# Routing a mixture of experts by comparing logits at once, with the common path behind the branch made the one that falls through

## The reference, cut to what matters

```python
def hierarchical_moe(h, w_rg, b_rg, w_re, b_re, w_e_gate, w_e_up, w_e_down):
    ...
    p_grp = jax.nn.softmax((t @ w_rg + b_rg).astype(jnp.float32), axis=-1)
    g_val, g_idx = lax.top_k(p_grp, 1)
    le = (t @ w_re + b_re).astype(jnp.float32).reshape(n, MOE_GROUPS, EXPERTS_PER_GROUP)
    le_sel = jnp.take_along_axis(le, g_idx[:, :, None], axis=1)[:, 0]
    p_exp = jax.nn.softmax(le_sel, axis=-1)
    e_val, e_idx = lax.top_k(p_exp, EXPERT_TOP_K)
    e_val = e_val / jnp.sum(e_val, axis=-1, keepdims=True)
    weight = g_val * e_val
    ...
```

## Time and profile before

| | |
|---|---|
| median of 3 runs | 1658.11 us (1657.22 to 1660.17) |
| profiled execution, first to last instruction | 1655.9 us |
| PE, DVE, ACT busy | 1530.4, 1093.5, 705.5 us |
| last xo matmul starts | 1392.08 us |
| first expert matmul starts | 1429.11 us |
| mean granted clock of TensorE | 0.988 |

### The profile page before, as it was taken

The page is one execution under the profiler, slowest core; times in us unless marked ns, Lnnn a source line. Parts: engine busy times, 40 slices in busy tenths (PEclk is TensorE's granted clock), DMA queues, the critical chain, the costliest instruction groups (busy, mean ns, idle before and its releaser), DMA issues.

```text
span 1655.9 us, 26753 instructions
## 1 busy us (share of the span) xinstructions
PE 1530.4 (92%) x11012; PEld 1284.9 (78%) x11012; DVE 1093.5 (66%) x1661; ACT 705.5 (43%) x1057; POOL 57.3 (3%) x52
## 2 busy tenths in 40 slices
PE   5999988998999999999999999999999888788892
PEld 4889777876878888888878787787898667788892
DVE  5831776686499637637689997455765445677775
ACT  5422444443344333323454222234344346367773
POOL 0000000000000000000000000000000000232121
PEclk9999999999999999999999999999999999999996
DMA  6220000002412222222312222232243103688995
GB/s 249 102 94 9 2 3 3 2 3 78 170 59 102 81 98 102 102 102 85 119 56 98 102 98 81 102 115 102 77 153 134 70 26 112 212 273 324 333 343 209
DMA packets 37832, 189.74 MB, mean 115 GB/s; under 512 B 4305, under 2 KB 4433, under 8 KB 24401
## 3 DMA queue, kind: packets, MB, share of 16 engines
q1 hardware_dynamic: 30672, 167.08, 28.1%
q0 software_dynamic: 4864, 16.78, 2.8%
q10 hardware_dynamic: 2176, 4.19, 0.8%
HBM read 175.46 MB, written 12.58 MB: 114 GB/s over the span
## 4 chain that ended last, share of the span: by engine, by line
PE 70%; DVE 17%; DMA 4%; ACT 4%; issue 3%; POOL 0%; SPq 0%; POOLq 0%; DVEq 0%; ACTq 0%
PE acc L474 18%; PE acc L476 18%; PE acc L475 18%; DMA raw<-wstream 3%; DVE CA L2439 2%; PE acc L725 2%; PE mb L725 1%; DVE wl L1958 1%; DVE wl L1970 1%; ACT wh L1254 1%; PE acc L1032 1%; PE mb L556 1%; DVE sqa L1887 1%; PE mb L610 1%; ACT wh L1267 1%
## 5 line engine op out<-in xcount | busy, mean ns | idle before, releaser
L474 PE MATMUL acc<-XH,wh 128*128 128x512 f32 x1008 | 396.3, 393 | 2.2 <-DVE wl L1970 1.3
L476 PE MATMUL acc<-XH,wl 128*128 128x512 f32 x1008 | 392.4, 389 | 0.0
L475 PE MATMUL acc<-XL,wh 128*128 128x512 f32 x1008 | 392.2, 389 | 0.0
L1267 ACT ACTIVATE wh<-raw 128x2048 fp32r<-128x2048 f32 x99 | 189.3, 1914 | 242.0 <-DMA raw<-wstream 242.0
L1970 DVE TENSOR_TENSOR wl<-raw,wh 128x2048 fp32r<-128x2048 f32 x99 | 226.1, 2287 | 67.2 <-ACT wh L1267 64.0
L474 PEld LDWEIGHTS acc<-XH,wh 128*128 128x128 f32 x1008 | 189.2, 188 | 44.6 <-issue 3.2
L475 PEld LDWEIGHTS acc<-XL,wh 128*128 128x128 f32 x1008 | 189.2, 188 | 40.8 <-issue 1.9
L476 PEld LDWEIGHTS acc<-XH,wl 128*128 128x128 f32 x1008 | 189.2, 188 | 39.6
L1288 ACT ACTIVATE ev<-acc 128x512 f32<-128x512 f32 x146 | 85.5, 597 | 216.7 <-PE acc L476 187.2
L1958 DVE TENSOR_TENSOR wl<-raw,wh 128x1024 fp32r<-128x1024 f32 x96 | 116.5, 1223 | 39.7 <-ACT wh L1254 39.3
L1254 ACT ACTIVATE wh<-raw 128x1024 fp32r<-128x1024 f32 x96 | 100.7, 1059 | 32.1 <-DMA raw<-wstream 31.7
(11 more groups left out here) (533 smaller groups left out, 2768.2 us busy)
## 6 DMA issues: line engine op xcount, KB each, us to landing
raw<-wstream SPq DMA_DIRECT2D x99, 1024.0 KB, 4.8
raw<-wstream SPq DMA_DIRECT2D x96, 512.0 KB, 6.1
YG<-YT ACTq DMA_DIRECT2D x8, 512.0 KB, 6.0
XT<-xT SPq DMA_DIRECT2D x2, 1024.0 KB, 9.7
XT<-xT SPq DMA_DIRECT2D x1, 2048.0 KB, 7.8
XD<-HN SPq DMA_DIRECT2D x4, 512.0 KB, 2.6
out<-XTK SPq DMA_DIRECT2D x4, 512.0 KB, 2.6
cst<-consts SPq DMA_DIRECT2D x1, 1230.0 KB, 18.5
```

The costliest lines, as they stand in the source:

```text
L474: mm(out_, a[0], b[0], start=start, stop=False)
L475: mm(out_, a[0], b[1], start=False, stop=False)
L476: return mm(out_, a[1], b[0], start=False, stop=stop)
L1267: actv(wh[:, n % RING].rearrange("p a b c -> p (a b c)"), raw[:, n % RING, :], ACT.Copy).then_inc(hi_done, 1)
```

## The change: what it does

1. **Routing.** All four-way comparisons of all 20 logits are made at once: differences `beat` (128x320), a comparison with a small tie-breaking constant, a sum that counts by how many an entry is beaten. Entries beaten by none (groups) or at most one (experts) are taken; `chosen` is the product of the two masks. No softmax is needed for it. The weights follow later from exponentials of the group logits and of the difference of the two experts' logits (`exponents` inside `place_first`, `two_weights` after `place(1)`). Weights for the dense path are made in that path.
2. **Last block of xo.** Tile 6 runs over all k, then routers 4 and 5, then tile 7. Tile 7 is added by DVE straight from PSUM. The low part of the third expert block of weights is made before tile 7 instead of after the choice.
3. **Transposes of the tokens.** They go in pairs of banks of `acc`, interleaved with the router; the first ones come before the logits' transposes, the last ones before the count. The stores to `XD` take two tiles of half the features each.
4. **Count and placing.** 6 matmuls for 14 in the count; `rows_in` of an expert is now cast before the next `G1` is begun; the flag is made after the first `G1`; the copies `pcur` go.
5. **Before the branch** only slot (0, 0) is turned and split, ahead of `slot_rows(1)`; the others follow one per block in `gathered(0)`, blocks 0 to 4. `keep_busy` there is 4 for 6.
6. **The branch.** Condition and bodies are swapped on PE, ACT and DVE: the common path falls through, the dense one is jumped to, and the common path jumps over it at its end. ACT's table for Silu is loaded before the branch.

```diff
-            for b in range(4):
+            for b in range(3):
                 stage_blocks("xo", 1, (s["xs_done"], 1) if b == 0 else None, start=b)
...
+            begin_block(n, t)
+            for j in range(2):
+                for k in range(KT):
+                    last = mm3(acc[:, (t + j) % 4, :], (wh[:, n % RING, k, j, :], wl[:, n % RING, k, j, :]),
+                               (XH[:, k, :], XL[:, k, :]), k == 0, k == KT - 1)
+                last.then_inc(acc_ready, 1)
+                if j == 0:
+                    router(4)
+                    router(5)
             router(6)
...
+            pe.wait_ge(s["rx_g"], 8)
+            for p in (2, 3):
+                pe.wait_ge(s["f_toke"], 2 * p - 2)
+                turned_row(p, 0)
+                turned_row(p, 1).then_inc(s["f_tok"], 2)
...
-            keep_busy(acc[:, 0, :], 10)
+            keep_busy(mb[:, 3, :], 5)
             slot_rows(0)
-            keep_busy(acc[:, 0, :], 12)
+            keep_busy(mb[:, 3, :], 10)
             pe.wait_ge(s["f_flag"], 1)
             crowded = pe.value_load(flag[0:1, 0:1])
+            turn_slots(0, 0)
             slot_rows(1)
-            turn_slots(0, 0)
-            turn_slots(0, 1)
-            with pe.If(crowded > 0):
+            with pe.If(crowded < 1):
+                gathered(0, first=True)
...
-                    if first and b < 4:
-                        slots_lower(b // 2, (2 + b) % 4)
+                    if first and b < 5:
+                        slots_lower(*divmod(b + 1, 4))
...
+            dve.wait_ge(acc_ready, T0["xo"] + 8)
+            link(v.tensor_tensor(XT[:, 7, :], XT[:, 7, :], acc[:, (T0["xo"] + 7) % 4, :], ALU.add))
...
+                link(v.tensor_tensor(beat[:, :, :, :], fours.unsqueeze(2).to_broadcast([P, TT * 5, 4, 4]),
+                                     fours.unsqueeze(3).to_broadcast([P, TT * 5, 4, 4]), ALU.subtract))
...
+                link(v.tensor_tensor(flat, flat, cs("tie").unsqueeze(1).to_broadcast([P, TT * 5, 16]), ALU.is_gt))
+                link(v.tensor_reduce(beaten[:, :, :, :].rearrange("p t s e -> p (t s) e"), beat[:, :, :, :], AX.X, ALU.add))
...
+                for e in range(4):
+                    v.tensor_tensor(G1[:, :, e, :], cs("count").unsqueeze(1).to_broadcast([P, TT, P]),
+                                    posn[:, 0, :, e:e + 1].to_broadcast([P, TT, P]), ALU.is_equal).then_inc(s["f_g"], 1)
...
+                    dve.wait_ge(s["f_count"], e + 2)
+                    v.tensor_copy(rows_in[:, e:e + 1], mb[:, e % 2, 2 * e:2 * e + 1]).then_inc(s["f_idx"], 1)
```

More of the change, by code:

```diff
@@ L426, in _ @@
             for n in range(99, 103):
[L427 to L431, removed]
+                load_halves(n, n % RING, early=n < 102)
+            for p in range(TT):
+                sp.wait_ge(s["f_toke"], 2 * p + 2)
+                t, c = 2 * (p % 2), slice(S * (p // 2), S * (p // 2) + S)
+                sp.dma_start(XD[t * P:(t + 2) * P, c].rearrange("(t p) d -> p t d", p=P),
+                             HN[:, t:t + 2, c]).then_inc(s["stored"], 16)
             load_range(103, 147)
@@ L1227, in _ @@
                     turn_rows(q)
[L1228 to L1232, removed]
         @block.scalar
@@ L1809, in gathered @@
                             act.dma_start(YG[h][:, q], src).then_inc((loaded_2nd if h else loaded)[q], 16)
[L1811 to L1821, removed]
+            act.wait_ge(rs_ready, NARROW[7])
+            for p in range(TT):
+                t, half = 2 * (p % 2), p // 2
+                act.wait_ge(s["f_tok"], 2 * p + 2)
+                for x in range(2):
+                    last = actv(HN[:, t + x, S * half:S * half + S], acc[:, t + x, :], ACT.Copy, scale=rs[:, t + x:t + x + 1])
+                last.then_inc(s["f_toke"], 2)
+            actv(sml[:, 61:62], cs("eps", 0, 1), ACT.Exp)
+            act.wait_ge(s["rt_sub"], 1)
+            actv(five_e[:, :, :], five[:, :, :], ACT.Exp).then_inc(s["rt_exp"], 1)
+            actv(sml[:, 62:63], cs("eps", 0, 1), ACT.Silu)
             act.wait_ge(s["f_flag"], 1)
@@ L1835, in _ @@
             chained = chain_n[0]
-            with act.If(crowded > 0):
+            with act.If(crowded < 1):
+                act.nop().then_inc(s["f_ye"], 1)
+                gathered(0, first=True)
+                with act.Fori(1, 3) as i:
+                    gathered(i)
+                gathered(3, last=True)
+                row_sums(0, 1)
+            chain_n[0] = chained
+            with act.Else():
                 for k in range(KT):
@@ L1848, in _ @@
                 row_sums(0, 2)
[L1849 to L1857, removed]
         @block.vector
@@ L2875, in _ @@
                 state.update(before)
+            with dve.Else():
+                all_weights()
+                dve.wait_ge(s["f_idx"], 8)
+                v.nop().then_inc(s["f_mask"], 1)
+                dve.wait_ge(s["stored"], 16 * TT)
+                v.nop().then_inc(s["f_idx"], 8)
+                for g in range(4):
+                    if g == 3:
+                        link(v.memset(YB[:, :, :, :], 0.0))
+                        v.nop().then_inc(s["f_ye"], 33)
+                    for e in range(4):
+                        dve.wait_ge(s[f"in_row{e}"], 16 * g + 16)
+                    if g < 3:
+                        v.nop().then_inc(s["f_tx"], 4 if g else 3)
+                for h in range(2):
+                    dve.wait_ge(s[f"y_out{h}"], 16 * 16)
+                operand(7, "norm_ffn")
+                loop(3, 16 + 8, lambda i: group("moe", i, 8))
+                group("moe", 3, 8, last=True)
+                for t in range(TT):
+                    final(t)
 def pack(inputs):
```

285 lines of the change are left out of this document (138 added, 147 removed).

## The result

The changed kernel takes 1672.91 us (median of 5 runs, 1668.04 to 1678.69), the kernel before 1660.17 in as many runs on the same chip (1657.22 to 1662.48): ratio 1.0085, 95% interval 1.0063 to 1.0106. It is slower by 0.85%, where 10.8 us less were forecast. The profiled execution spans 1673.0 us, against 1655.9.

What follows compares the result with a forecast made beforehand. The chain from last xo to first expert matmul (37.0 us) was taken as the bound the change works on: 11.6 us saved there, less 0.8 given back, 10.8 off the 1655.9 span, median 1647.3 us; range 1643.8 to 1652.0.

Steps and rivals of the forecast that it cites:

- that stretch: The 37.0 us between the last xo matmul (1392.08) and the first expert matmul (1429.11).
- the rivals: Stall at the branch stays (0.12, 1651.1 us); experts' stretch takes more back (0.10, 1649.4); first gather late (0.04, 1655 to 1658).
- The one slower case: In the experts, the clock stays at half for over 5 blocks; 6 blocks give 1664 us; chance 0.02.
- Step 1: Last tile to logits: routers 4 and 5 move ahead of tile 7, shifts nearly cancel, 0.1 us saved.
- Step 2: Logits to the choice: seven operations instead of some 35, 2.6 us for 8.5, 6.0 us saved.
- Step 3: Choice to places (`posn`): 2.05 us instead of 4.05, the count held by ACT's scaling, 2.0 us saved.
- Steps 4 to 6: Places to experts: row numbers 2.1 us lost; `G1` end 0.7 saved; rows, branch and dummies 4.9 saved.
- step 4: Places to the last row numbers: each expert a closed round of 1.55 us, about 6.8 us, 2.1 us lost.
- The half clock during the 20 dummies: Ahead of the experts: a stretch at half clock makes dummies, turning and rows end some 1.9 us later.
- Step 7: In the experts: one more slot turned and split inside group 0, 0.8 us given back, bounds 0 and 1.3.
- over 228 us from the first expert matmul to the end: Sign of a wrong prediction: this stretch longer than 228 us, with 226.8 before and 227.6 expected.
- Step 8: The end: the common path's jump over the dense path costs 0, with 1.3 us kept for the range.

Runs made afterwards that it cites:

- kernel 3: The changed kernel with `tie` and `picks` written by memsets into scratch, `rank` kept in `cst`, so tiles stay at the old addresses: 1650.59 us, ratio 0.9943.
- experiment 6: TensorE's branch turned round: kernel 3 with the old way, 1656.77 us, ratio 0.9966; the kernel before with the new way, 1658.89 us, ratio 0.9993.
- experiment 4: kernel 3 with 24 dummy matmuls behind the last expert matmul on PE, ahead of the jump at the end: 1650.96 us, ratio 0.9954.
- `after_gap`: The changed kernel with a further 128-byte hole ahead of XT, so XT to `ar` lie 256 bytes higher than before: 1651.29 us, ratio 0.9953.
- experiments 4 and 7: The second of these is `after_gap` without the last eight dummies ahead of the experts: 1651.23 us, ratio 0.9936.

## Why the prediction was wrong

**The step that failed** is the premise ahead of the steps: "The change works on that stretch and nothing else". It left out a term, the 32 columns in `cst`, that lies in none of the eight steps: 18.8 us up to the last xo matmul between the profiled executions of the changed kernel and kernel 3, 21.0 in the old kernel with 32 columns more, about twice the forecast gain. None of the rivals had it. The one slower case, at 0.02, was the clock in the experts; the real one came in the first 1392 us, in instructions that both kernels have in the same order.

**The steps themselves**, read where the tiles lie as before (kernel 3, its DVE and PE timelines), against the forecast. Rows go from start to start of an instruction, where the forecast counts from ends; that shifts up to 0.2 us between neighbours.

| stage, us | forecast | kernel 3 | changed kernel |
|---|---|---|---|
| last xo matmul to logits (before 6.78) | 5.3 | 4.99 | 5.39 |
| logits to `chosen` (before 8.5) | 2.6 | 2.40 | 2.40 |
| `chosen` to `posn` (before 4.3) | 2.05 | 2.33 | 3.25 |
| `posn` to the last row number (before 4.5) | 6.8 | 6.28 | 7.10 |
| to the end of `G1` (before 4.0) | 3.15 | 3.21 | 3.21 |
| to the experts (before 8.97) | 4.1 | 4.04 | 4.05 |
| sum (before 37.0) | 24.0 | 23.25 | 25.40 |

- *Step 1* held: routers 4 and 5 cost the 1.4 us that they were given, and the shorter way behind tile 7 gives them back.
- *Step 2* held to 0.2 us; the operations on 320 elements take the 0.49 us that was read off the line through the earlier trace rows.
- *Step 3* held in kernel 3, where the granted clock is 1.00 while PE turns the tokens, and is 1.2 us short in the changed kernel. There it was 0.50 from 1420 to 1423 (the row of 3.65 us for 20 transposes); I had all of it at full clock. The count comes late, and DVE waits 2.51 us for it.
- *Steps 4 to 6* held. The terms of step 4 add up to 7.1 us and not to the 6.8 that were used; 6.28 were measured. The half clock during the 20 dummies came as foreseen (0.66 from 1412 to 1417 in kernel 3). The branch fell through in 88 to 92 ns, and experiment 6 shows in both directions that its standing is a price of the jump. The Trainium skill, in Advanced Engine Details and Errata, section Control Flow Timing, has about 108 ns for a compare-and-branch, and doesn't say which way. The 92 ns are near that, and the 5531 ns of the same branch laid the other way are not.
- *Step 7*: 0.8 us given back can't be told. From the first expert matmul to the last matmul whose result is used it takes 196.4 us before, 199.0 in kernel 3, 194.4 in experiment 4 and 194.9 in `after_gap`. Two kernels that differ by 24 dummies at the very end lie 4.6 us apart. The prediction named over 228 us from the first expert matmul to the end as a sign of being wrong: the profile of the changed kernel has 232.0, with the wait of 3.74 us in it, its repeat 228.5, kernel 3 230.4 and `after_gap` 226.3, so this sign varies with the execution by more than the term that it was to test.
- *Step 8* was 0, with 1.3 kept for the range. The jump takes 3.3 to 4.3 us of PE's sequencer (5.6 behind the dummies of experiment 4), and dummies ahead of it change nothing. The part behind the last matmul is 1.0 us longer than before (30.4 us) in kernel 3 and `after_gap`, and 1.9 in experiments 4 and 7, which is over the bound.

The forecast gain was 10.8 us. With the tiles at the old addresses it is 8.8 us, and 256 bytes higher 9.8 (1659.34 - 1650.59 and 1661.1 - 1651.29). That the sum comes out so near owes something to luck: the lull gave 12.4 us instead of 11.6 (13.8, less the 1.4 of the routers), while each stretch of lower clock ahead of it costs about 1.5 us, of which these executions have two or three, and the part behind it varies by 4 (226.3 to 230.4). The range, too, was wider than its terms, which reach from 1645.4 to 1648.8 and not from 1644.5 to 1649.5. Four versions of the changed kernel, at 1650.6 to 1651.3 us, are faster than both the kernel before and the one of the diff.

## What to carry to other kernels

Read a diff for what it does to addresses, too: a column more in a tile that is placed ahead of others moves all of them. Before any theory about the code that was changed, look for the first place at which the traces part; if it lies ahead of the change, compare the mean spacing of one kind of instruction in code that both share. And take away a stall together with what is next in line: the same branch, turned round, was worth nothing that the runs could tell in the old order and 4 to 5 us in the new one.

## What the runs showed that I had not expected

- A float32 128x512 matmul starts on average every 0.2267 us where its streamed operand lies as before or 256 bytes higher, every 0.2289 us 64 bytes higher, and every 0.2324 to 0.2333 us 128 bytes higher. That is up to 2.9% on the largest term of this kernel. Other distances were not tried, nor were `wh` and `wl`, the stationary operands of these matmuls, moved.
- 128x256 matmuls that stream `wh` go the other way when their stationary operand is moved: 0.1200 us before, 0.1186 at 128 bytes and 0.1134 at 64, 5.5% less. Why the two shapes differ is open.
- The Trainium skill, in TensorE: Matmul & The Clock Gate, section Step-by-step: what each phase is for, has the throughput as one column per cycle and names no address; an estimate from it at 2.4 GHz is 0.213 us for 512 columns. The 0.2267 to 0.2333 us of the runs differ from that in the size and in that they hang on the address.
- The same skill, in SBUF — State Buffer, section Operand start alignment, asks for a multiple of the element size and says of its own runs that this is "about legality, not speed". All kernels here keep to it, and the runs above add the speed.
- Standing 3.55 us at a jump cost 0.9 us more in the dummies behind it and 1.1 in the expert matmuls, at a granted clock of 0.50.
